# A two-block transformer kernel: dilated attention of a head pair placed between the projection tiles of the next pair, and a delta-rule step opened one step early

## What is computed

```python
def dilated_mixer(u, w_qkv, q_gain, k_gain, w_o):        # 3 dilations, 16 heads of 64
    qkv = (u @ w_qkv).reshape(b, s, N_DIL, 3, N_HEADS, HEAD_DIM)
    for g in range(N_DIL):
        q = rope(rms_norm(qkv[:, :, g, 0], q_gain[g]))
        k = rope(rms_norm(qkv[:, :, g, 1], k_gain[g]))
        o, lse = dilated_attention(q, k, qkv[:, :, g, 2], DIL_WINDOWS[g], DIL_RATES[g])
        ...
    w = softmax(stack(lses), axis=0)
    return sum(w * stack(outs)) @ w_o
```

## Time and profile before

| what | us |
|---|---|
| median of 3 runs | 4119.39 |
| the profiled execution | 4121.26 |
| its span, first to last instruction | 4119.3 |
| mean granted TensorE clock | 0.948 |
| PE busy | 3773.0 (92%) |
| DVE busy | 1771.8 (43%) |
| ACT busy | 1345.9 (33%) |

### The profile page before, as it was taken

How to read it: one execution, slowest core, us unless ns; L and a number is a source line. 1 busy time by engine, 2 the same in 40 slices (tenths; PEclk the granted TensorE clock), 3 DMA queues, 4 the chain that set the end, 5 groups by cost and what they waited for, 6 DMA issues and landing times.

```text
span 4119.3 us, 48890 instructions
## 1 busy us (share of the span) xinstructions
PE 3773.0 (92%) x18780; PEld 2926.7 (71%) x18780; DVE 1771.8 (43%) x3745; ACT 1345.9 (33%) x2422; POOL 85.7 (2%) x166
## 2 busy tenths in 40 slices
PE   8879999989999998888888889999799997889999
PEld 3459955578887886777777757886688865556887
DVE  4657635455454334444444433332233326453333
ACT  1141111332233223555555533222122225352222
POOL 1000001000000000000000000000000000000000
PEclk9979999989998999999999999999799988899999
DMA  6400027335442222111111102222222220002222
GB/s 244 179 1 1 1 95 270 139 141 179 179 156 104 82 95 76 55 47 57 52 47 62 57 32 96 97 87 85 86 77 108 79 77 1 21 1 95 90 102 72
DMA packets 47133, 362.61 MB, mean 88 GB/s; under 512 B 5216, under 2 KB 5600, under 8 KB 28000
## 3 DMA queue, kind: packets, MB, share of 16 engines
q1 hardware_dynamic: 23616, 272.47, 18.0%
q0 software_dynamic: 23328, 87.50, 6.0%
HBM read 357.86 MB, written 2.10 MB: 87 GB/s over the span
## 4 chain that ended last, share of the span: by engine, by line
PE 83%; DVE 6%; issue 4%; ACT 3%; PEld 1%; DVEq 1%; DMA 0%; PEldq 0%; ACTq 0%; SPq 0%
PE bank L802 18%; PE bank L808 18%; PE bank L807 18%; PE bank L754 11%; PE bank L1409 4%; PE bank L733 2%; PE bank L688 2%; PE bank L712 2%; PE bank L783 1%; PE bank L583 1%; PE bank L595 1%; PE bank L1939 1%; PE bank L702 1%; DVE work_sb L1802 1%; PE bank L560 1%
## 5 line engine op out<-in xcount | busy, mean ns | idle before, releaser
L802 PE MATMUL bank<-x_hi_sb,w_hi_sb 128*128 128x512 f32 x2336 | 918.5, 393 | 57.6 <-issue 23.4
L807 PE MATMUL bank<-x_lo_sb,w_hi_sb 128*128 128x512 f32 x2336 | 914.9, 392 | 0.0
L808 PE MATMUL bank<-x_hi_sb,w_lo_sb 128*128 128x512 f32 x2336 | 914.4, 391 | 0.0
L966 ACT ACTIVATE w_hi_sb<-slab_sb 128x1024 fp32r<-128x1024 f32 (+2 forms) x476 | 424.3, 921 | 405.3 <-PE bank L802 225.8
L802 PEld LDWEIGHTS bank<-x_hi_sb,w_hi_sb 128*128 128x128 f32 x2336 | 442.3, 189 | 154.0 <-issue 45.8
L1119 DVE TENSOR_TENSOR w_lo_sb<-slab_sb,w_hi_sb 128x1024 fp32r<-128x1024 f32 (+2 forms) x476 | 484.0, 1055 | 108.2 <-ACT w_hi_sb L966 96.1
L808 PEld LDWEIGHTS bank<-x_hi_sb,w_lo_sb 128*128 128x128 f32 x2336 | 442.3, 189 | 93.3
L807 PEld LDWEIGHTS bank<-x_lo_sb,w_hi_sb 128*128 128x128 f32 x2336 | 442.6, 189 | 91.7
L1197 DVE TENSOR_TENSOR hid_sb<-silu_gate_sb,bank 128x512 f32<-128x512 f32 x110 | 75.6, 687 | 654.0 <-PE bank L808 654.0
L802 PE MATMUL bank<-hid_hi_sb,w_hi_sb 128*128 128x512 f32 x880 | 342.7, 389 | 0.0
L808 PE MATMUL bank<-hid_hi_sb,w_lo_sb 128*128 128x512 f32 x880 | 342.4, 389 | 0.0
(11 more groups left out here) (284 smaller groups left out, 4380.5 us busy)
## 6 DMA issues: line engine op xcount, KB each, us to landing
slab_sb<-weights SPq DMA_DIRECT2D x81, 2048.0 KB, 7.8
slab_sb<-weights SPq DMA_DIRECT2D x44, 1536.0 KB, 6.4
keep_sb<-ada POOLq DMA_DIRECT2D x94, 512.0 KB, 4.5
work_sb<-ada POOLq DMA_DIRECT2D x54, 512.0 KB, 5.4
slab_sb<-weights SPq DMA_DIRECT2D x20, 1280.0 KB, 5.9
tables_sb<-ada POOLq DMA_DIRECT2D x12, 512.0 KB, 5.6
tables_sb<-tables POOLq DMA_DIRECT2D x1, 2496.0 KB, 9.2
h_sb<-x SPq DMA_DIRECT2D x4, 512.0 KB, 7.3
```

Of the source, the lines that this page charges most:

```text
L802: mm = pe.matmul(bank[s][:, :], w_hi[p][:, w], hi, start=first, stop=False)
L807: pe.matmul(bank[s][:, :], w_hi[p][:, w], lo, start=False, stop=False)
L808: return pe.matmul(bank[s][:, :], w_lo[p][:, w], hi, start=False, stop=last)
L966: e.eng.activation(w_hi[p][:, 0:cols], e.raw[:, quarter * cols:(quarter + 1) * cols], ACT.Copy).then_inc(w_hi_ready, 1)
```

## The change

**Dilated stage.** A slot is now the 9 projection tiles of one pair with the attention of the pair before it. After every tile, PE runs three numbers m of a list (`between(m)`, m = 0 to 26); each m holds at most one piece of the value products, one of the transposes, one of the scores, and some sums. The first slot has no attention, the last no projection. ACT and DVE have matching orders written by hand. The rings are new: 3 banks for projection tiles, 1 for the attention output, 2 for scores, spreads and sums (before: 2 and 4), one buffer for swapped halves (before: 2). A unit's scores of 512 keys take both score banks, the 2x128 keys take them again. The factors are spread straight from the 48 columns, 64 columns wide, for keys only; the query's factor is now the `scale` operand of the mask instruction, which therefore works on 512, 128 and 128 columns in place of 512 and 256, and a second maximum is taken. `d_rep`, L721, L712 and three of the six multiplications go. The root is moved: sums are kept after each dilation (`keep_sums`), and root and reciprocal run beside the end of a slot. Sqrt and Exp tables are still loaded once each per pair.

```diff
+        def pe_dilated(e, par, project=True, attending=True):
...
+            def between(m):
+                if attending:
+                    if m in (1, 2):
+                        spread(m - 1)
+                    if m == 2:
+                        spread(2)
+                        turn_values(2)
+                    u, k = divmod(m - 10, 3)
+                    if 0 <= u < NB:
+                        values(u, k)
+                    u, k = divmod(m - 8, 3)
+                    if 0 <= u < NB:
+                        turn(u, k)
+                    u, k = divmod(m - 3, 3)
+                    if 0 <= u < NB and k < 2:
+                        scores(u, k)
+                    if m == 21:
+                        pe.drain().then_inc(dil_out.full[e.out_now], 1)
+                if project:
+                    if m in (8, 18, 26):
+                        sums()
+                    if m in (22, 23):
+                        turn_values(m - 22)
...
+                for m in range(3 * t, 3 * t + 3):
+                    between(m)
...
+            mask(0)
+            rope(0, 0)
+            w_lo_part(4)
+            weigh(0)
+            mask(1)
+            w_lo_part(5)
+            rope(0, 1)
+            keep_sums(0)
+            value_tile()
+            weigh(1)
+            mask(2)
+            w_lo_part(6)
+            weigh(2)
+            mask(3)
+            rope(1, 0)
+            w_lo_part(7)
+            weigh(3)
...
+            values_turned(0)
+            act_table(e, ACT.Sqrt)
+            swap_in(2, 1)
+            values_turned(1)
+            w_hi_part(12)
...
```

```diff
             for step in range(NB):
...
                 for w in ways:
+                    if more:
+                        decays(w, step + 1)
                     w.used(pe, step, "rky")
                     each(w, step, "v_new", (of(w.Y), of(w.RV)), (of(w.A), of(w.S)))
                 for w in ways:
+                    if more:
+                        betas(w, step + 1)
+                for w in ways:
                     w.used(pe, step, "v_new")
+                    pe.wait_ge(w.blocks, 2 * step + 2)
                     each(w, step, "o", (of(w.S), of(w.QG)), (of(w.X), of(w.QK)))
                     each(w, step, "state", (of(w.KG), of(w.X)))
```

More of the change, by code:

```diff
@@ L704, in pe_spread @@
             mm.then_inc(e.A.full[s], 1)
[L706 to L723, removed]
         def pe_slab_opening(e, x, ready):
@@ L1312, in two_blocks @@
         sqf = sq[:, :, :].rearrange("p a b -> p (a b)")
-        DN_USES = ["g", "kk", "qk", "beta", "eG", "turn",
-                   *(f"{x}{lv}" for lv in range(1, LEVELS) for x in ("AXY" if lv < LEVELS - 1 else "AY")),
-                   "rky", "v_new", "o", "state"]
+        DN_LEVELS = [f"{x}{lv}" for lv in range(1, LEVELS) for x in ("AXY" if lv < LEVELS - 1 else "AY")]
+        DN_USES = {}
+        for step in range(-1, NB):
+            uses = [(step, x) for x in ("qk", "turn", *DN_LEVELS, "rky")] if step >= 0 else []
+            if step < NB - 1:
+                uses += [(step + 1, x) for x in ("g", "kk")]
+            if step >= 0:
+                uses += [(step, "v_new")]
+            if step < NB - 1:
+                uses += [(step + 1, "beta")]
+            if step >= 0:
+                uses += [(step, x) for x in ("o", "state")]
+            for x in uses:
+                DN_USES[x] = len(DN_USES)
         class Way:
@@ L1495, in act_delta @@
                     last.then_inc(w.sides, 1)
+            decays(0)
+            for step in range(NB):
+                sides(step)
                 for w in ways:
@@ L1539, in dve_delta, with opening @@
             eyes = ident.unsqueeze(1).to_broadcast(full)
-            for step in range(NB):
+            def opening(step):
                 noted = [0, 0]
@@ L1915, in pe_run @@
             e.stage_end("dilated_norm")
[L1917 to L1934, removed]
-                    pe.wait_ge(squared, e.nth(squared))
-                    for x in range(2):
-                        for b in range(NB):
-                            at = 2 * ((3 * x + g) * NB + b)
-                            mm = pe.matmul(e.S.bank[cols][:, at:at + 2],
-                                           d_sq[:, 2 * (g % 2) + x, b * P:(b + 1) * P], K("head2"),
-                                           start=True, stop=True)
-                    return mm
-                for g in range(3):
-                    pe_parts(e, 3, KT, x_hi, x_lo)
-                    if g:
-                        sums(g - 1)
-                sums(2).then_inc(e.S.full[cols], 1)
-                for j in (0, 3, 1, 4, 2, 5):
-                    pe_spread_heads(e, j)
-                pe.wait_ge(heads_ready, e.nth(heads_ready))
-                attend(e, dilated_units(), 1, None, d_buffers)
@@ L2182, in act_run @@
[L2182 to L2189 removed]
+            e.use(e.dil)
@@ new lines, in act_run @@
+            act_table(e, ACT.Exp)
+            act_dilated(e, first=True)
+            with repeat(act, PAIRS // 2 - 1, [*e.rates(slab=6, acc=18, tp=30, maxed=8, pv_done=24, cols_kept=6),
+                                              (e.halves, 12), (e.part, 24), (e.out, 2)]) as n:
+                for x in range(2):
+                    act_dilated(e, out=d_y[:, 2 * n + x, :])
+            act_dilated(e, last=True, out=d_y[:, PAIRS - 2, :])
+            act_dilated(e, project=False, out=d_y[:, PAIRS - 1, :])
```

471 lines of the change are left out of this document (344 added, 127 removed).

## The result

| | before | after |
|---|---|---|
| median of 5 runs, us | 4121.37 (4119.14 to 4124.59) | 4098.27 (4093.06 to 4102.20) |
| profiled execution (its span) | 4121.3 (4119.3) | 4093.06 (4091.2) |

The ratio is 0.9943, 95% interval 0.9929 to 0.9958: faster by 23 us, where 67 were forecast. The time lies 3 us above the range.

A forecast was written before the change was run, and what follows sets the result against it. PE was taken to bound the dilated stage and to be busy most of the delta steps. 4121.3 less 55.1 (dilated stage) and 10.6 (delta stage) gave 4055.6, less 1.9 for the median: 4054 us, range 4000 to 4095.

The forecast's parts named there:

- Clock: Dilated stage: slots run mostly at full clock; half-speed products only at cold start and two loop turns (1.9 and 7.2 us).
- The rival: Dilated slots: clock falls where PE has little to do; two per slot 4077 us, three or four up to 4100; chance 0.19.
- Pieces: Dilated slot: transposes 6.8, value products 5.9, scores 6.0 us, plus 0.15 us at each of nine changes of operand.
- Waits: Dilated slot: PE still waits for score banks, weight parts 7 and 12 and the sums' bank, together 8.7 us.
- The two of 0.8: Units 3 and 4 of a slot's attention, counted from 1: 0.8 us lost in each before the second score group.
- Spreads, first slot and end: Dilated stage: spreads 3.0 us per slot, first slot to the end of tile 7 49.1, end without projection 52.5.
- Scale operand: DVE masks in the dilated stage: a scale from memory costs 0 to 0.06 us each, taken as 0.
- Table load: ACT in the dilated slot: Sqrt load takes 1.28 us, next instruction 0.02 later, without the skill's extra drain of about 1.38.
- Delta stage: Delta steps: opening 22.5 us for 25.3 at three openings (8.4), 2.2 at the first; sum 10.6 us less.
- "Slower" in eight places: Dilated slots: clock falls in every attention gap and mid tile 5, 13.2 us per slot, 4146 us; chance 0.04.
- "a part late by 8 us": Dilated slot: a weight part some 8 us late in a misread order, no gain there, 4107 to 4119; chance 0.03.
- "Fewer waits": Dilated slots: DVE and ACT run ahead, full-latency waits too many; 3993 us at none, 4023 at half; chance 0.22.

The follow-up runs named there:

- grouped: Changed kernel with the three value pieces of a gap between tiles issued in a row, ahead of its transposes and scores; 4113.46 us, ratio to before 0.9968 to 0.9986.
- four reorderings of single pieces: Changed kernel with two second score groups in the next tile, weight parts 7 and 12 made earlier, column sums moved from gap 2 to gap 3; 4041.46 us.

## Why the prediction was wrong

The forecast for the stage was 715.0 us, and it took 761.7: 46.7 more. By its own terms:

- **Clock (the step that failed first).** The forecast allowed slow products at the cold start and at the two turns of the loop alone, some 25. There were 160, so 135 x 0.20 = 27 us. The rival had the mechanism, both of its main places (gap 2; behind the wait for w_lo) and its price of 1.65 us; with 20 runs in seven slots, three per slot, it gave "up to 4100". That the time came out there is partly luck: the falls cost 27 us, not the 35 to 46 that lead to "up to 4100", and much of the rest is the next term, which no rival had. It got 0.19 on the strength of one row: attention at clock 1.00 with "four waits of 1.0 us". The four are 1.01, 1.03, 1.20 and 0.78 us, and that stretch has no two-column sums and none of the later waits of 1.62 and 2.43. The step that failed is this one: "since the slot runs mostly at full clock". The granted clock of the stage was 0.94, where "0.98 or more" was forecast for the loop.
- **Pieces.** "0.15 us at each of nine changes of operand" counted the changes between products and pieces. Inside a gap the kinds alternate, and each change costs about as much: 12 value pieces by 0.10, 12 transpose pieces by 0.12, four score units by 0.21 are 3.5 us a slot. The accounted slot (1688.63 to 1780.68) has 32.4 us of pieces for 28.8: 3.6 x 7 = 25 us. grouped shows the price, 0.49 for 0.58.
- **Waits (right).** 1.62, 1.62, 0.35, 0.49, 2.43, 0.6 and 0.3 are 7.4 us, forecast 8.7: 9 us back over seven slots. The two of 0.8 came out shorter, with slower pieces between the groups. At the two turns of the loop the wait is 1.1 us longer than in other slots, where 2.0 was forecast: 2 us more back.
- **Spreads, first slot and end.** The spreads took 2.9 for 3.0; the first slot ended 1.1 us later and the end took 54.9 for 52.5.
- Together 27 + 25 - 11 + 3.5 = 44.5 of the 46.7; some 2 us stay open.
- **Scale operand (wrong, small).** Taken as 0 from bounds of 0 to 0.06; it was 0.06 for each of twelve, all on the path, 5 us. They lie inside the measured waits above.
- **Table load (right).** 1.28 us, and the next ACT instruction starts 0.01 later:

```profile
1773.13 1.28 ACT L906 ACT_TABLE_LOAD   x1
1774.42 0.20 ACT L906 ACTIVATE small_sb<-small_sb 128x1 f32<-128x1 f32 x1
```

  The extra drain that the Trainium skill gives (ScalarE: Activation LUTs, What ACT_TABLE_LOAD costs) isn't there in this kernel either.
- **Delta stage (opening right, sum wrong by the same step).** From rky to the first level 22.5 us, forecast 22.5, at three openings:

```profile
461.70 1.49 PE L1411 MATMUL bank<-sq_sb,work_sb 128*128 128x128 f32 x11
...
484.22 3.14 PE L1411 MATMUL bank<-sq_sb 128*128 128x128 f32 x13 [1.75 <-DVE sq_sb L1604]
```

  That is 8.3 us of the 8.4. The first opening gave 0.9 for 2.2. But the stage gave 4.9 us for 10.6, since the six levels of products that follow an opening ran slower, in all four steps together 134.3 us in place of 130.0. The sum had them at their old price. The levels of the last step, before and after:

```profile
491.43:524.05 32.62, 32.62 (x273) 32.05 (x273) 23.90 (x35) 0.00 (x0) 0.00 (x0) 0.96 0.00 1
...
484.22:518.33 34.11, 34.11 (x273) 33.54 (x273) 23.90 (x35) 0.00 (x0) 0.00 (x0) 0.92 0.00 1
```

  The work is the same and PE never waits in either; the granted clock is 0.92 for 0.96. Ahead of the levels of a later step PE now waits 1.38 and 1.75 us, where it waited 3.52 and then at most 0.41; that this brings the clock down isn't shown. The eleven kernels with this delta stage all take 227.7 to 228.3 us for it, the two without it 233.1 and 235.1.
- **Median.** The 1.9 us by which the median was put below the profiled execution were noise: five runs gave 4121.37.
- **Rivals.** "Slower" in eight places didn't come; "a part late by 8 us" neither. "Fewer waits" was wrong too: taken at full latency the waits were right.

What makes the clock fall is not settled. Shown is that neither the wait nor the pieces suffice as a rule, that moving 1.7 us of two-column products from one gap to the next is worth 20 us, and that the same pieces and waits are followed by a fall in some slots and not in others. Why gap 3 bears the sums and gap 2 doesn't isn't shown, and that the moment at which a slot starts has a part in it is a rival that no run tests.

## What to carry to other kernels

Cutting an attention into the gaps of a projection hides it, but count each change between kinds of small matmul as 0.1 to 0.15 us (the price here), and try the matmuls of few columns and the waits in different gaps. After such a change count the products at half speed, by place: here they were 27 of the 47 us that were missing, and four reorderings of single pieces gave 57 us, of which 136 fewer slow products are 27 and shorter waits most of the rest. Do the same for a stage whose waits alone were changed: the delta steps lost half of their gain in products that nobody had touched. Before moving a piece of PE's away from a wait, ask whether another engine sets the end of that wait: then the piece was hidden there.

## What was not expected of the hardware

- With the sums moved to gap 3, waits of 1.62, 1.62 and 2.44 us within one slot left the granted clock at 1.00 in the slot shown, and five of the seven slots had no slow product in tiles 2 to 5; with them in gap 2, the same waits go with 0.76 in tile 3.
- Removing the wait inside tile 5 went with slow products in tile 2 in all seven slots in place of two (1.62 us wait unchanged, clock 0.77).
- The mask instruction takes 60 ns longer with its scale in memory, whatever its size: 747 for 687 at 512 columns, 347 for 286 at 128.
